# Value products of the forgetting attention on column halves of TensorE, transposed back one step later

## The reference

```python
def fox_attention(q, k, v, log_f):
    F = jnp.cumsum(log_f, axis=-1)
    ...
        logits = (jnp.einsum('bhqd,bhkd->bhqk', qi, kf) * scale
                  + Fi[..., :, None] - F[:, :, None, :])
        logits = jnp.where(kpos[None, :] <= qpos[:, None], logits, -jnp.inf)
        p = jax.nn.softmax(logits, axis=-1)
        return jnp.einsum('bhqk,bhkd->bhqd', p, vf)
```

## Time and profile before

| | us |
|---|---|
| median of 3 runs | 1638.18 (1638.09 to 1639.43) |
| the profiled execution | 1638.64 |
| its span | 1636.8 |
| TensorE matmul busy | 1611.1 |
| VectorE busy | 885.2 |
| ScalarE busy | 636.3 |
| GpSimd busy | 238.8 |
| the stage, first transposition of step 3 to first product of `xs0` | 42.74 |

### The profile page before, as it was taken

One profiled execution on the slowest core, in us unless ns is written; L12 is line 12 of the kernel. 1 busy time (PEld: TensorE's weight loads), 2 busy tenths in 40 slices (PEclk: granted clock), 3 DMA queues, 4 the chain that ended last, 5 costly groups with the idle time before them and its releaser, 6 DMA issues.

```text
span 1636.8 us, 19219 instructions
## 1 busy us (share of the span) xinstructions
PE 1611.1 (98%) x7584; PEld 1274.7 (78%) x7584; DVE 885.2 (54%) x1447; ACT 636.3 (39%) x1089; POOL 238.8 (15%) x216
## 2 busy tenths in 40 slices
PE   7999999999999999999999999999999999999998
PEld 5567788876767888888888887786788888888887
DVE  6556456755477455333433324578555677777322
ACT  4332124446455433322232222456563344444222
POOL 1323302400031134111010203000013200000000
PEclk9999999999999999999999999999999999999999
DMA  8121113221211332233233322411103232322322
GB/s 278 39 77 40 52 56 104 91 77 52 65 52 54 116 102 91 90 103 103 91 102 94 100 90 73 168 65 39 53 1 104 90 101 83 99 92 90 129 91 77
DMA packets 39733, 142.12 MB, mean 87 GB/s; under 512 B 4531, under 2 KB 5299, under 8 KB 39260
## 3 DMA queue, kind: packets, MB, share of 16 engines
q1 hardware_dynamic: 39644, 140.89, 26.7%
HBM read 138.76 MB, written 2.11 MB: 86 GB/s over the span
## 4 chain that ended last, share of the span: by engine, by line
PE 89%; DVE 4%; POOL 3%; ACT 2%; issue 1%; DMA 0%; SPq 0%; POOLq 0%; ACTq 0%; DVEq 0%
PE ps L406 86%; PE ps L409 3%; POOL sqs L2147 2%; POOL sqt L2145 1%; DVE wlo L916 1%; ACT whi L1558 1%; DVE uT L1080 0%; DVE uT L1078 0%; DMA x<-in_x 0%; PE ps L902 0%; ACT PT L1883 0%; ACT zb L1868 0%; DVE raw L1129 0%; POOL small L2039 0%; DVE W L1371 0%
## 5 line engine op out<-in xcount | busy, mean ns | idle before, releaser
L916 DVE TENSOR_TENSOR wlo<-wraw,whi 128x1024 fp32r<-128x1024 f32 (+2 forms) x244 | 304.4, 1251 | 451.8 <-ACT whi L1558 451.3
L406 PE MATMUL ps<-hThi,whi 128*128 128x512 f32 x1128 | 455.6, 404 | 0.8 <-DVE sqT L1446 0.8
L1558 ACT ACTIVATE whi<-wraw 128x1024 fp32r<-128x1024 f32 (+2 forms) x244 | 252.2, 1038 | 486.6 <-PE ps L406 455.6
L406 PE MATMUL ps<-hThi,wlo 128*128 128x512 f32 x1128 | 440.5, 391 | 0.0
L406 PE MATMUL ps<-hTlo,whi 128*128 128x512 f32 x1128 | 440.0, 390 | 0.0
L406 PEld LDWEIGHTS ps<-hThi,whi 128*128 128x128 f32 x1128 | 212.2, 188 | 60.7 <-issue 20.1
L406 PEld LDWEIGHTS ps<-hThi,wlo 128*128 128x128 f32 x1128 | 212.0, 188 | 45.3
L406 PEld LDWEIGHTS ps<-hTlo,whi 128*128 128x128 f32 x1128 | 212.4, 188 | 44.6 <-issue 3.6
L406 PE MATMUL ps<-whi,hThi 128*128 128x512 f32 (+1 forms) x224 | 86.7, 387 | 0.0
L406 PE MATMUL ps<-whi,hTlo 128*128 128x512 f32 (+1 forms) x224 | 84.1, 376 | 0.0
L406 PE MATMUL ps<-wlo,hThi 128*128 128x512 f32 (+1 forms) x224 | 84.0, 375 | 0.0
(11 more groups left out here) (310 smaller groups left out, 2430.7 us busy)
## 6 DMA issues: line engine op xcount, KB each, us to landing
wraw<-in_ws SPq DMA_DIRECT2D x236, 512.0 KB, 3.5
x<-in_x SPq DMA_DIRECT2D x4, 512.0 KB, 4.9
x<-in_x SPq DMA_DIRECT2D x1, 2048.0 KB, 9.9
Fb<-forget_rows SPq DMA_DIRECT2D x1, 2048.0 KB, 8.2
out<-ys SPq DMA_DIRECT2D x8, 256.0 KB, 2.4
w<-in_w SPq DMA_DIRECT2D x2, 512.0 KB, 12.2
dec<-in_dec SPq DMA_DIRECT2D x1, 1024.0 KB, 14.8
wraw<-in_ws SPq DMA_DIRECT2D x4, 256.0 KB, 2.5
```

Source lines behind the costliest of these rows:

```text
L406: return t.matmul(o, l, r, start=first, stop=last)
L916: v.tensor_tensor(wlo[h][:, 0:width(i)], wraw[h][:, 0:width(i)], whi[h][:, 0:width(i)].bitcast(F32), ALU.subtract).then_inc(lo_done[h], 1)
L1558: a.activation(whi[h][:, 0:width(i)], wraw[h][:, 0:width(i)], ACT.Copy).then_inc(hi_done[h], 1)
```

## The change

A call of `values` now serves two units, every second step (even u, for units u-6 and u-5). The weights are 64 columns of `fv`, the 128 columns of `PTf` move, the first head's result goes to PSUM partitions 0 to 63 and the second's to 64 to 127. The result is thus transposed (head dimension by query), so a row block, once its eight heads are done, is copied to SBUF by ScalarE (`heads_out`, into `W5[0]`, `W5[1]`, `W5[2]`), transposed back by TensorE (`back`, four transpositions, signal `x_bk`) and only then divided by the row sums. The pieces of the norm stand later: `out_norm_turn` of q = 4 and 5 at steps 24 and 28 in place of 22 and 26, and the last row block is turned back behind the first slot of `xs0`. In a step the scores now come behind `turn` and `values`, save in steps 4 and 6, and on ScalarE `evac` comes ahead of `shares`.

```diff
--- before.py
+++ after.py
@@ -341,8 +341,8 @@
     s_mk = sem("s_mk")
     s_qk, s_z, s_ab, s_ln, s_sc, s_sum, s_tr, s_ev, s_pv = (
         sem(n) for n in ("s_qk", "s_z", "s_ab", "s_ln", "s_sc", "s_sum", "s_tr", "s_ev", "s_pv"))
-    x_qk, x_mx, x_ex, x_tr, x_ea, x_ev, x_pv, x_nv = (
-        sem(n) for n in ("x_qk", "x_mx", "x_ex", "x_tr", "x_ea", "x_ev", "x_pv", "x_nv"))
+    x_qk, x_mx, x_ex, x_tr, x_ea, x_ev, x_pv, x_bk, x_nv = (
+        sem(n) for n in ("x_qk", "x_mx", "x_ex", "x_tr", "x_ea", "x_ev", "x_pv", "x_bk", "x_nv"))
     o_c, o_sq, o_sc, o_tr, o_hi, o_lo = (sem(n) for n in ("o_c", "o_sq", "o_sc", "o_tr", "o_hi", "o_lo"))
     w_y, w_r, w_0, w_1 = (sem(n) for n in ("w_y", "w_r", "w_0", "w_1"))
 
@@ -799,31 +799,50 @@
                 free[b] = [(x_ea if u % 2 else x_ev, u // 2 + 1)]
 
             def values(u):
+
                 n, h = pairs[u]
                 b = 6 if n > 1 else 7
-                w.wait_ge(x_ea if u % 2 else x_ev, u // 2 + 1)
+                w.wait_ge(x_ev, u // 2 + 1)
+                w.wait_ge(x_ea, u // 2 + 1)
                 w.wait_ge(fv_c, 4)
                 if h == 0:
                     take(b)
                 for k in range(n + 1):
-                    op = mm(ps[b][:, h * 64:(h + 1) * 64], PTf[u % 4][:, k * 128:(k + 1) * 128], fv[:, k, h * 64:(h + 1) * 64],
-                            k == 0, k == n)
-                op.then_inc(x_pv, 1)
-                if h == 7:
-                    free[b] = [(x_nv, 2 * (13, 15, 29, 31).index(u) + 2)]
+                    for i in range(2):
+                        op = mm(ps[b][64 * i:64 * i + 64, h * 64:h * 64 + 128], fv[:, k, (h + i) * 64:(h + i + 1) * 64],
+                                PTf[(u + i) % 4][:, k * 128:(k + 1) * 128], k == 0, k == n)
+                        if k == n:
+                            op.then_inc(x_pv, 1)
+                if u == 30:
+                    free[b] = [(o_c, 8)]
+
+            def back(q, b):
+
+                w.wait_ge(o_c, 5 + q)
+                if b == 1:
+                    take(b)
+                for k in range(4):
+                    op = across(b, k, W5[q % 3][:, k * 128:(k + 1) * 128])
+                op.then_inc(x_bk, 1)
+                free[b] = [(x_nv, 2 * q + 2)]
 
             for u in range(38):
                 while u == 3 and not fox_go:
                     yield
-                if u < 32 and u % 2 == 0:
+                if u in (4, 6):
                     scores(u)
                 if 3 <= u < 35:
                     turn(u - 3)
-                if u in (7, 22, 26):
-                    out_norm_turn({7: 3, 22: 4, 26: 5}[u], 3)
-                if 5 <= u < 37:
-                    values(u - 5)
-                yield
+                if u in (7, 24, 28):
+                    out_norm_turn({7: 3, 24: 4, 28: 5}[u], 3)
+                if u in (20, 22, 36):
+                    back((20, 22, 36).index(u), 7 if u == 22 else 6)
+                if u >= 6 and u % 2 == 0:
+                    values(u - 6)
+                if u < 32 and u % 2 == 0 and u not in (4, 6):
+                    scores(u)
+                yield
+            flow.later(1, lambda: back(3, 1))
             flow.later(1, lambda: out_norm_turn(6, 3))
             flow.later(2, lambda: out_norm_turn(7, 3))
 
@@ -1409,13 +1428,13 @@
 
             def shares(q, n):
                 u = (13, 15, 29, 31)[q]
-                c, b = 48 + 8 * n, 6 if n > 1 else 7
+                c, b = 48 + 8 * n, (6, 7, 6, 1)[q]
                 w.wait_ge(x_ex, u + 1)
                 if q:
                     w.wait_ge(x_nv, 2 * q)
                 v.reciprocal(st2[:, 40:48], st2[:, c:c + 8]).then_inc(x_nv, 1)
                 w.wait_ge(x_nv, 2 * q + 1)
-                w.wait_ge(x_pv, u + 1)
+                w.wait_ge(x_bk, q + 1)
                 w.wait_ge(o_sc, 3 * (4 + q))
                 w.wait_ge(o_sq, 4 + q)
                 v.tensor_tensor(heads(W5[3][:], 8), heads(ps[b][:], 8), st2[:, 40:48].unsqueeze(2).to_broadcast([128, 8, 64]),
@@ -1430,12 +1449,13 @@
                     evac(u - 3)
                 if u == 8:
                     out_norm_low(3, 0, "gsb", 3)
-                if u in (23, 27):
-                    out_norm_low(4 + u // 27, 4, "gfox", 3)
-                if u - 5 in (13, 15, 29, 31):
-                    q = (13, 15, 29, 31).index(u - 5)
-                    shares(q, (3, 0, 2, 1)[q])
-                yield
+                if u in (25, 29):
+                    out_norm_low(4 + u // 29, 4, "gfox", 3)
+                if u in (20, 22, 36):
+                    q = (20, 22, 36).index(u)
+                    shares(q, (3, 0, 2)[q])
+                yield
+            flow.later(1, lambda: shares(3, 1))
             flow.later(1, lambda: out_norm_low(6, 4, "gfox", 3))
             flow.later(2, lambda: out_norm_low(7, 4, "gfox", 3))
 
@@ -1919,23 +1939,35 @@
                     w.wait_ge(x_pv, u - 3)
                 a.activation(PTf[u % 4][:, 0:wd], ps[4 + u % 2][:, 0:wd], ACT.Copy).then_inc(x_ea, 1)
 
+            def heads_out(q, u):
+
+                w.wait_ge(x_pv, u + 1)
+                if q == 3:
+                    w.wait_ge(x_bk, 1)
+                a.activation(W5[q % 3][:], ps[7 if q % 2 else 6][:], ACT.Copy).then_inc(o_c, 1)
+
+            def finished(q):
+                w.wait_ge(x_nv, 2 * q + 2)
+                out_norm_square(4 + q)
+
             for u in range(38):
                 while u == 3 and not fox_go:
                     yield
+                if 3 <= u < 35 and (u - 3) % 2:
+                    evac(u - 3)
                 if u < 32:
                     shares(u)
-                if 3 <= u < 35 and (u - 3) % 2:
-                    evac(u - 3)
                 if u == 7:
                     out_norm_high(3, 0, "gsb", 3)
-                if u in (22, 26):
-                    out_norm_high(4 + u // 26, 4, "gfox", 3)
-                if u - 5 in (13, 15, 29, 31):
-                    q = (13, 15, 29, 31).index(u - 5)
-                    w.wait_ge(x_nv, 2 * q + 2)
-                    out_norm_square(4 + q)
+                if u in (24, 28):
+                    out_norm_high(4 + u // 28, 4, "gfox", 3)
+                if u in (18, 20, 34, 36):
+                    heads_out((18, 20, 34, 36).index(u), u - 5)
+                if u in (20, 22, 36):
+                    finished((20, 22, 36).index(u))
                 yield
             flow.later(1, lambda: out_norm_high(6, 4, "gfox", 3))
+            flow.later(1, lambda: finished(3))
             flow.later(2, lambda: out_norm_high(7, 4, "gfox", 3))
 
         none = lambda b, p, done: None
@@ -2186,8 +2218,8 @@
             for u in range(38):
                 while u == 3 and not fox_go:
                     yield
-                if u in (5, 20, 24, 36):
-                    out_norm_scale({5: 3, 20: 4, 24: 5, 36: 6}[u])
+                if u in (5, 22, 26, 37):
+                    out_norm_scale({5: 3, 22: 4, 26: 5, 37: 6}[u])
                 yield
             flow.later(1, lambda: out_norm_scale(7))
 
```

## The result

| | before | changed |
|---|---|---|
| median (lowest to highest, runs) | 1639.03 us (1638.09 to 1639.45, 6) | 1643.74 us (1643.07 to 1646.27, 6) |
| the profiled execution | 1638.64 | 1643.74 |
| its span | 1636.8 | 1641.6 |
| first transposition of the stage, from the span's start | 1177.97 | 1178.45 |
| the stage | 42.74 | 46.47 |

The ratio is 1.0031, with a 95% interval from 1.0021 to 1.0041: slower by 0.3%. The stage has 3.73 us of it and the projection 0.49; the stage also began 0.48 later, which lies within what no changed instruction explains (over the eleven profiled executions of this study it began between 1177.38 and 1179.78).

A forecast was written before the change was run, and what follows sets the result against it. TensorE bounds the kernel, busy 1611.1 of 1636.8 us. Products -4.9, transpositions +1.8 and waits +7.4 give +4.3 on 1638.64, that is 1642.9; the median lies 0.46 lower, so 1642.5 us, range 1635.6 to 1646.5.

The forecast's parts named there:

- Value products, gain 4.9: TensorE's value products in the forgetting attention's stage: 11.3 us on column halves instead of 16.2, a gain of 4.9.
- Turning back, 1.8: 16 added transpositions on TensorE at 0.11 us, 1.8 us in all, with four ScalarE copies at 0.57.
- Waits, 7.4: Added TensorE waits in the stage, as less work covers the path through VectorE and ScalarE: 7.4 us in sum.
- T of 25 and 29: Transpositions of units 25 and 29, behind exponential, four gain copies, exponential and copy on ScalarE: waits 0.75 us each, 1.5.
- T of 8 and 9: Transpositions of units 8 and 9, behind VectorE's minimum, four residuals, minimum and copy: waits 0.7 and some 0.4, 1.1 us.
- T of 30 and 31: Transpositions of units 30 and 31, with no more scores issued and VectorE late from residuals: 0.5 us each, 1.0.
- The covers hold: First rival, in the stage: other engines run ahead enough, waits under 1.2 us, 4.5 us gone, 1633.7 us; chance 0.15.
- half the waits: Rival, in the stage: waits of 3.7 us, as one wait lets other engines catch up; 1638.8 us, no change; chance 0.28.
- The halves run side by side: Opposite of a rival on the value products: each of 80 pairs costs 0.22 instead of 0.11, 1647.6 us; chance 0.05.
- (a): Claim tested by the follow-up experiments, on the stage: the loss is the order, scores last; no size or chance given.
- (b): Claim tested by the follow-up experiments, on the stage: the loss is the turning back and its waits; no size given.
- (c): Claim tested by the follow-up experiments, on the value products: they gain little; no size or chance given.

The follow-up runs named there:

- Experiment 4: The kernel before, with its old value products and no turning back, put in the change's order (values of two units together, scores last, `evac` before exponential): 1642.57 us.
- Experiment 8: The kernel of experiment 2 run once more, unaltered: 1642.35 us, ratio 1.0018 to the kernel before.
- Experiment 1: The changed kernel with TensorE's scores back at the head of every even step, all else kept: 1639.79 us, ratio 1.0000 to the kernel before.
- experiment 2: The changed kernel with the copy of the finished row block ahead of ScalarE's exponential in steps 18 and 20: 1642.64 us, ratio 1.0020 to the kernel before.

## Why the prediction was right

Forecast 1642.5 us, slower; measured 1643.74, slower. The forecast's stage, summed from its terms, was 42.74 - 4.9 + 1.3 + 7.4 = 46.5; it was 46.47. The projection was to be 0.44 longer and was 0.49. The missing 1.2 us of the total lie ahead of the stage (0.48), around the span (0.3) and in the 0.46 that was taken off for the median.

**Value products, gain 4.9.** Stage 46.47 less 7.48 us of waits is 38.99, that before less its 0.40 of waits 42.34. The 3.35 between them and the 1.3 that the turning back added make 4.7, under the 4.9 by 0.2. Experiment 4 comes to the same: the form gave 5.4, and the order took 0.7 of pace. The forecast took both in one step, from the calls as they stood before to those of the window attention. The window attention's row gave the pace of a pair correctly (1.03 for n = 3, as worked out), and the direct step from column to row halves cost what was taken: the last pair of that call starts at 1187.42 and the scores 0.21 later, priced at 0.20.

The Trainium skill, "TensorEngine Tiling (Array Packing)", section Theoretical Speedup, says up to two times for such operands. The records alone come near it at four key blocks (1.83 to 1.03, 1.8 times) and not at one (0.49 to 0.37, 1.3 times). Of the 7.0 us that the records gained in this stage, the entries took 1.6 and the turning back with its waits 4.9.

**Turning back, 1.8.** As priced: 0.44 of pace and 0.58 of copy each, of which three groups of the four stand in the stage.

**Waits, 7.4.** One by one, forecast and measured:

| wait | forecast | measured | how |
|---|---|---|---|
| first turning back | 1.0 | 1.03 | above |
| second | 1.5 | 1.49 | above |
| third | 0.8 | 0.78 | 1223.74 - 1222.15 - 0.81 |
| T of 25 and 29 | 1.5 | 1.68 | 1213.64 - 1212.47 - 0.33, twice |
| T of 8 and 9 | 1.1 | 1.08 | above |
| T of 30 and 31 | 1.0 | 0.87 | 1221.12 - 1220.13 - 0.59; 1221.81 - 1221.12 - 0.22 |
| small ones | 0.5 | 0.55 | 0.18 at scores(6); 1195.32 - 1194.17 - 0.98; 1208.50 - 1207.76 - 0.54 |

Sum 7.5. The last of the small ones is values of n = 1 behind a turning back, until the division has read their bank. The terms came out one by one, not only in their sum, since each was walked through the queue of the engine that releases it, with the durations of the trace before. The largest group outside the turning back shows that chain as it was forecast, on ScalarE:

```profile
1210.90 0.62 ACT L1932 ACTIVATE Tf<-Tf,st 128x384 f32<-128x384 f32 x1 [0.83 <-DVE st L1419]
...
1211.51 1.12 ACT L1873 ACTIVATE ohi<-ps,vec 128x128 fp32r<-128x128 f32 x4
1212.51 0.62 ACT L1932 ACTIVATE Tf<-Tf,st 128x384 f32<-128x384 f32 x1
...
1213.11 0.39 ACT L1940 ACTIVATE PTf<-ps 128x256 f32<-128x256 f32 x1
```

The copy ends at 1213.50 and TensorE's T of unit 25 starts at 1213.64, 0.14 later, as in the earlier trace rows.

The sum is closer than its terms. The kernel before had 0.4 us of waits of its own, so 7.1 were added where 7.4 were forecast, and the products gained 4.7 where 4.9 were; that these two misses nearly cancel, to 0.1 us in the stage, is luck.

**The rivals.** "The covers hold" and "half the waits" both fall by this table: a wait at one place did not pay for the next. Experiment 8 has a piece of the second in it (0.70 of 2.52 came back as another wait). Experiment 1 shows that with the scores in front the covers nearly hold (1.2 us of waits left); but its total only came back to that of before, as the second switch took what the first rival would have gained. The halves run side by side (16 records in 1.03).

**What the prediction left unsaid.** It put the loss on waits, and did not part the order from the form. Experiments 1 and 4 do: (a) holds, the order costs 3.0 us by itself and putting it back takes 4.4 off the changed stage; (b) holds too, 4.9; they overlap, since scores in front also cover the first two turnings back (2.5). (c) falls: the form gains 5.4. Nor did it see that each place of the scores has its price in switches.

## What to carry to other kernels

Before speeding up an engine's filler work, list what that work was covering: here products that were 5.4 us shorter, together with scores issued last, exposed 7 us of a path through two other engines that had cost 0.4 us of waiting before. A result that comes out transposed costs more than its transposition: 0.44 us of TensorE and 0.58 of ScalarE came with a wait of up to 1.5 us where the copy was queued behind an operation that itself waited, so put such copies ahead of it, and turn back only the blocks that are long enough to pay. Price a tiled form with its switches, and look at which neighbours it gets in the order. And add up waits from start to start: the view of waits listed 5.6 of 7.5 us here, and a wait inside a merged row is easily taken for slower work.

## What was not expected of the hardware

The clock: in one of two profiled executions of the same program (experiments 2 and 8), TensorE had 0.50 of its clock for 6.8 us, from about 1220.1 us on; in the 2 us before it had been busy for 1.38. In the other execution TensorE was busy for 1.40 and 1.28 us in the 2 us stretches from 1220 and 1222 on, and the clock stayed at 1.00, as it did in the profiled execution of the changed kernel, which waited longer. The stage was 1.6 and the projection 1.2 us longer in the first, 2.75 us in all. Such a stretch takes 0.002 off the mean clock of a whole execution. A mean of 0.997 stands beside one more of the ten executions of experiment 2 (1643.65 us), beside none of the ten of experiment 8, and beside one of the six of the changed kernel (1646.27, its longest); apart from one execution of the kernel before (0.949, 1646.64 us) all others have 0.999 or 1.000. What set it off stays open; that the program alone does not is shown.

The price of a switch also varied with its place: going over from full rows to row halves cost 0.14 to 0.15 in experiment 1, where the trace before had shown 0.09 on the same step behind value products; from full rows to column halves 0.10. And 16 value records in a row were 0.06 slower than twice 8 with a transposition between. These are small, but 12 to 16 of each make 1 to 2 us of a stage of 42.
